# Sixteen of a layer's 32 modulation products moved from the convolution stage into the state-space chunk loop

## What is computed

```python
mod = (jax.nn.silu(c) @ w['w_ada'] + w['b_ada'])[:, None, :]     # w_ada: 1024 x 6144
sh1, sc1, g1, sh2, sc2, g2 = jnp.split(mod, 6, axis=-1)
h = rmsnorm(x, w['ln_mix']) * (1 + sc1) + sh1
q, k, v, qi, ki, wi, z, xbc, dtr, xpool = _split_cols(h @ w['w_in'], IN_SIZES)
a_out = attend(q, k, v, qi, ki, wi)
s_out, new_ssm, new_conv = ssd_mixer(z, xbc, dtr, ...)           # width-4 convolution, chunked state-space scan
p_out, new_pool = pool_mixer(xpool, ...)
x = x + g1 * (jnp.concatenate([a_out, s_out, p_out], axis=-1) @ w['w_out'])
h2 = rmsnorm(x, w['ln_ffn']) * (1 + sc2) + sh2
x = x + g2 * ((jax.nn.silu(h2 @ w['w_gate']) * (h2 @ w['w_up'])) @ w['w_down'])
```

## Time and profile before

| | us |
|---|---|
| median of 3 runs | 3644.96 (3644.76 to 3650.87) |
| the profiled execution | 3638.68 |
| span of its records | 3636.9 |
| mean granted TensorE clock, share of full speed | 0.922 |

### The profile page before, as it was taken

The page is one execution under the profiler, slowest core; times in us unless marked ns, Lnnn a source line. Parts: engine busy times, 40 slices in busy tenths (PEclk is TensorE's granted clock), DMA queues, the critical chain, the costliest instruction groups (busy, mean ns, idle before and its releaser), DMA issues.

```text
span 3636.9 us, 58311 instructions
## 1 busy us (share of the span) xinstructions
PE 3195.1 (88%) x20553; PEld 2728.6 (75%) x20553; DVE 1590.9 (44%) x3481; ACT 1181.4 (32%) x2077; POOL 258.2 (7%) x319
## 2 busy tenths in 40 slices
PE   3997787788889999999989877877888999999995
PEld 2995533265889999999979744334568999999994
DVE  3425568974342222322353265888634323222223
ACT  3222247764332212112131222686532321211211
POOL 1001032102000000000000102210020000000000
PEclk8998779897989999999989976999979999999997
DMA  5125035303311111111122232440151111111111
GB/s 184 38 43 197 21 106 174 105 2 122 111 35 46 42 51 45 41 48 45 41 49 45 87 142 83 139 157 7 48 169 41 41 44 49 46 42 51 46 41 48
DMA packets 275989, 261.18 MB, mean 72 GB/s; under 512 B 85512, under 2 KB 237566, under 8 KB 274512
## 3 DMA queue, kind: packets, MB, share of 16 engines
q1 hardware_dynamic: 244496, 155.76, 14.3%
q0 software_dynamic: 31312, 103.20, 8.8%
HBM read 249.33 MB, written 9.78 MB: 71 GB/s over the span
## 4 chain that ended last, share of the span: by engine, by line
PE 77%; DVE 8%; issue 6%; ACT 4%; DMA 3%; DVEq 0%; another core or an unknown queue 0%; POOL 0%; ACTq 0%; SPq 0%; POOLq 0%
PE bank L723 55%; PE bank L686 5%; PE bank L760 3%; DMA weights<-in_w_ada 2%; ACT arena L1444 2%; PE bank L1123 2%; PE bank L1097 2%; DVE arena L1938 2%; PE bank L1186 1%; PE bank L971 1%; DMA arena<-in_x_sample 1%; PE bank L1145 1%; PE bank L833 1%; PE bank L1063 1%; PE bank L739 1%
## 5 line engine op out<-in xcount | busy, mean ns | idle before, releaser
L723 PE MATMUL bank<-h_hi,w_hi 128*128 128x352 f32 x2784 | 903.2, 324 | 4.5 <-DVE w_lo L1567 4.5
L723 PE MATMUL bank<-h_lo,w_hi 128*128 128x352 f32 x2784 | 893.1, 321 | 0.0
L723 PE MATMUL bank<-h_hi,w_lo 128*128 128x352 f32 x2784 | 892.3, 321 | 0.0
L723 PEld LDWEIGHTS bank<-h_hi,w_hi 128*128 128x128 f32 x2784 | 522.8, 188 | 6.9 <-issue 5.1
L723 PEld LDWEIGHTS bank<-h_lo,w_hi 128*128 128x128 f32 x2784 | 523.6, 188 | 1.7
L723 PEld LDWEIGHTS bank<-h_hi,w_lo 128*128 128x128 f32 x2784 | 522.4, 188 | 0.0
L1567 DVE TENSOR_TENSOR w_lo<-weights,w_hi 128x1024 fp32r<-128x1024 f32 x188 | 230.2, 1225 | 609.6 <-ACT w_hi L1267 603.7
L723 PE MATMUL bank<-g_hi,w_hi 128*128 128x352 f32 x1392 | 451.1, 324 | 5.5 <-DVE arena L629 5.5
L723 PE MATMUL bank<-g_lo,w_hi 128*128 128x352 f32 x1392 | 448.1, 322 | 0.0
L723 PE MATMUL bank<-g_hi,w_lo 128*128 128x352 f32 x1392 | 447.6, 322 | 0.0
L686 PEld LDWEIGHTS bank<-arena 128*128 128x128 f32 (+4 forms) x1773 | 218.1, 156 | 239.3 <-issue 184.3
(11 more groups left out here) (330 smaller groups left out, 3725.7 us busy)
## 6 DMA issues: line engine op xcount, KB each, us to landing
weights<-in_w_ada SPq DMA_DIRECT2D x64, 512.0 KB, 6.8
weights<-in_w_gate SPq DMA_DIRECT2D x44, 512.0 KB
weights<-in_w_up SPq DMA_DIRECT2D x44, 512.0 KB, 3.8
weights<-in_w_in SPq DMA_DIRECT2D x72, 256.0 KB, 3.5
arena<-in_w_ada SPq DMA_DIRECT2D x32, 512.0 KB
weights<-in_w_down SPq DMA_DIRECT2D x32, 448.0 KB, 3.6
arena<-in_w_ada SPq DMA_DIRECT2D x8, 1024.0 KB, 18.2
weights<-in_w_down SPq DMA_DIRECT2D x16, 512.0 KB, 3.8
```

The costliest lines, as they stand in the source:

```text
L723: mm = pe.matmul(bank[:, 0:TC], wt[:, w], xt[:, x], start=(k + m == 0), stop=(k == n_k - 1 and m == 2))
```

## The change

Stage 4 keeps the first sixteen loads (row 1), and ScalarE copies them out after all four Silus and not between the second and third. The other sixteen (row 2) are multiplied in stage 5, two behind the `outputs` of each of the eight full chunks, the last two of them ahead of the transposes of the final state. They accumulate in a bank of their own, `GB`, which is bank 2; the ring `A` has only banks 0 and 1 in that stage. Row 2 is copied out and turned at the end of stage 5, through another place in SBUF (`O_ADAT2`). TensorE's loop of three turns over pairs of chunks becomes straight code. SyncE's program is the same: it issues a load as soon as the buffer six loads ahead is free. VectorE's and GpSimd's programs stay as they were.

```diff
-        AB_FEW, DB_MORE = psum[0:2], psum[2:6]
+        AB_FEW, DB_MORE, GB = psum[0:2], psum[2:6], psum[2]
-        O_ADAT = R(23, 512)
+        O_ADAT, O_ADAT2 = R(23, 512), R(25, 512)
...
-                for u in range(ADA_EARLY):
-                    if u == 2 * KD:
-                        pe.wait_ge(ada_rows, l * 3 + 2)
-                        modulation_turn(l * 3 + 2)
+                def modulation_part(u, into=YB):
+
                     pe.wait_ge(ada_full[u % 6], l * (16 * ((ADA_EARLY + 5 - u % 6) // 6)) + 16 * (u // 6 + 2))
-                    modulate(O_ADAE[u % 6], u // 2 % KD, u % 2).then_inc(w_empty, 1)
-                modulation_turn(l * 3 + 3)
+                    modulate(O_ADAE[u % 6], u // 2 % KD, u % 2, into).then_inc(w_empty, 1)
+
+                for u in range(2 * KD):
+                    modulation_part(u)
+                modulation_turn(l * 3 + 2)
...
                 Dr.restart()
+                A.use(AB_FEW)
                 decays(0, 0, P, C("upper"), C("ones"))
                 settle(pe)
-                with loop(pe, NB // 2 - 1, counts) as i:
-                    for t in range(2):
-                        decays(i * 2, t + 1, P, C("upper"), C("ones"))
-                        outputs(i * 2, t)
-                decays(0, NB - 1, P, C("upper"), C("ones"))
-                outputs(0, NB - 2)
+                for c in range(NB - 1):
+                    if c % 2 == 0 and c < NB - 2:
+                        Dr.pos = 3
+                    decays(c - c % 2, c % 2 + 1, P, C("upper"), C("ones"))
+                    outputs(c - c % 2, c % 2)
+                    for u in range(2):
+                        modulation_part(2 * KD + 2 * c + u, GB)
...
                 outputs(0, NB - 1)
+                for u in range(2):
+                    modulation_part(4 * KD - 2 + u, GB)
                 Dr.wait_read()
...
-                A.restart()
+                modulation_turn(l * 3 + 3, O_ADAT2)
+                A.use(AB)
                 ended(pe, l, 5)
...
                     act.activation(S(R(R_U + i), TOK), S(R(R_U + i), TOK), ACT.Silu)
-                    if i == 1:
-                        modulation_rows(w_empty, l * ADA_USES + 2 * KD)
-                        modulation_columns(1)
-                modulation_rows(w_empty, l * ADA_USES + 4 * KD)
-                modulation_columns(2)
+                modulation_rows(w_empty, l * ADA_USES + 2 * KD)
+                modulation_columns(1)
...
                 exponentials(0, NB, NS)
-                A.restart()
+                modulation_rows(w_empty, l * ADA_USES + 4 * KD, GB, O_ADAT2)
+                modulation_columns(2)
+                A.use(AB)
                 ended(act, l, 5)
```

More of the change, by code:

```diff
@@ L765, in pair_by_tile, with modulate, modulation_turn @@
                 units.n += 2
-            def modulate(at, k, h):
+            def modulate(at, k, h, into=YB):
                 for j in range(4):
-                    mm = pe.matmul(B(YB, [[1, 256]], 256 * h, 32 * j, 32), S(O_CT + 32 * k, 32), S(at + 256 * j, 256),
+                    mm = pe.matmul(B(into, [[1, 256]], 256 * h, 32 * j, 32), S(O_CT + 32 * k, 32), S(at + 256 * j, 256),
                                    start=(k + h == 0), stop=(k + h == KD), skip_group_check=True)
                 return mm
-            def modulation_turn(rows):
+            def modulation_turn(rows, at=O_ADAT):
                 pe.wait_ge(ada_rows, rows)
@@ L779, in modulation_turn @@
                 for c in range(4):
-                    mm = T(B(bank, [[1, P]], P * c), S(O_ADAT + P * c, P))
+                    mm = T(B(bank, [[1, P]], P * c), S(at + P * c, P))
                 A.close(mm)
@@ L1309, in _, with modulation_rows @@
             act.activation(S(R(1), D, 0, 9), S(R(1), D, 0, 9), ACT.Silu).then_inc(c_silu, 1)
-            def modulation_rows(sem, done):
+            def modulation_rows(sem, done, bank=YB, at=O_ADAT):
                 act.wait_ge(sem, done)
-                act.activation(S(O_ADAT, 512), YB[:, :], ACT.Copy).then_inc(ada_rows, 1)
+                act.activation(S(at, 512), bank[:, :], ACT.Copy).then_inc(ada_rows, 1)
             def modulation_columns(r):
```

## The result

The changed kernel takes 3620.86 us (median of four runs, 3618.26 to 3621.77) where the kernel before takes 3647.05 (3644.76 to 3650.87): ratio 0.9926, 95% interval 0.9911 to 0.9942, 26 us less. The changed kernel's profiled execution has a span of 3619.9 us, only 17.0 less than the 3636.9 of before, so 9 of the 26 us are not in this pair of traces at all. Much of what follows is about them.

The account below looks back on a forecast made before the run. TensorE had 77% of the chain, with `w_ada` loads ending stage 4 and ScalarE's staging awaited in stage 5; 9.7 + 6.5 - 0.7 - 2.0 = 13.5 us less, 3625.2 profiled, 3631.5 timed, range 3621 to 3641.

Parts of the forecast that it names:

- The leg of loads: End of stage 4: `w_ada` loads with modulation end last; moving sixteen leaves VectorE's convolution and pooling as the late leg.
- From the mark to the first `decays`: End of stage 4: 0.2 us from VectorE's mark to the first pooling product, then 6.75 to ScalarE's staging, both layers.
- The loads in stage 5: Stage 5: added parts wait for loads in TensorE's queue, but six buffers cover them; costed at nothing.
- rivals C and D: Stage 5 chunk loop: C, TensorE bounds the chain, 3645 us, chance 0.10; D, its clock falls, 3658, chance 0.04.
- 6.5 less 0.7: Stage 5 chunk intervals: filled gaps raise TensorE's clock, 6.5 us gained, less 0.7 for added parts in slow intervals.
- the changed kernel's should stand likewise: Timed runs: the median stands 6.3 us above the profiled execution, so profiled 3625.2 becomes timed 3631.5.
- the term of stage 4: End of stage 4: pooling products begin right behind VectorE's mark; 3.4 us gained in layer 1, 6.3 in layer 2, together 9.7.
- The term with the wrong sign: End of stage 5: parts 30 and 31 ahead of the state's transposes cost 1.0 us in each layer, 2.0 together.
- The added parts at half clock: Stage 5 gaps: two added parts per chunk cost 0.15 us for each interval still at half clock.
- rival D: Stage 5 chunk loop: added parts push it to half clock, 13 us slower, 3658 us; chance 0.04.

Follow-up runs that it names:

- `e_unroll`: The kernel before with only TensorE's loop over pairs of chunks written out as straight code; no product moved or added; ratio to before 0.9997.
- `e_fill_only`: The kernel before, stage 4 untouched, chunk loop as straight code, two modulation parts with unread results behind each chunk's outputs; ratio to before 0.9962.

## Why the forecast was half of the gain

**What was right.** The leg of loads ended stage 4, and VectorE's took its place. From the mark to the first `decays` I had 6.95 us to the staging and so 7.8 to `decays`, 15.6 for both layers; three traces have 15.8 in the mean. The loads in stage 5 hold nobody up. The gap had room: rivals C and D did not come. The clock rose with the added work and gave 7.0 us in the first pair of traces, 8.2 in the mean of all, where 6.5 less 0.7 was forecast. The straight code gives nothing.

**The step that failed: "the changed kernel's should stand likewise".** The profiled execution of before lay 6.3 us under the median of its timed runs and 6.1 under the fastest of them, and I carried the 6.3 over to the changed kernel as an offset common to both. It isn't common. The changed kernel's profiled execution (3621.77) is the highest of its four timed runs, 0.9 us above their median of 3620.86. The forecast for the profiled execution, 3625.2, was 3.4 us too high; the forecast for the timed runs, 3631.5, was 10.6 too high, and 7.2 of these are this step.

Where the first trace of before saved its time isn't settled. Against the three later traces it has 25.3 us from mark to first `decays` in place of 31.6, 30.9 and 30.6. Its clock over that stretch was 0.80 and 0.61, theirs 0.59 to 0.64, and its pooling products began 5.8 and 6.5 us behind VectorE's mark, theirs 7.7 to 8.8. In the changed kernel they begin 0.2 us behind it in every trace, and the whole stretch takes 7.3 to 8.5 us a layer, so what the loads added, and what they varied by, is gone. By the means of all traces the term of stage 4 is 13.8 us where 9.7 were forecast. The longer stretch of the three later traces would account for some 6 us if the timed runs of before on the slower kind of chip had it as well; no trace from such a chip does (25.3, and 23.4 in `e_unroll`). Nor did a low trace save its time in these stages alone: the one of `e_unroll` has a span 7.9 us under that of the first trace of before, and in stages 4 and 5 it is 2.2 us longer.

**The term with the wrong sign: the end of stage 5.** I added 2.0 us for parts 30 and 31 ahead of the state's transposes. From `L922` to `L686` it is 2.28 us in layer 1 and 3.02 in layer 2, where 1.85 were before; so the parts did cost 0.4 and 1.2, near enough. But the whole end got 2.2 shorter in the mean, and the clock was still up when it began: the eight products of the sample chunk's `decays` took 1.07 and 1.08 us (`L905`), and 1.91 and 1.73 before (`L904`). TensorE's timeline in layer 1, before and after:

```profile
430.40 1.91 PE L904 MATMUL bank<-arena 32*128 32x32 f32 x8
424.10 1.07 PE L905 MATMUL bank<-arena 32*128 32x32 f32 x8
```

I had let the gain of the clock end with the sixth interval. `e_fill_only`, with the added products alone, has the end 4.2 us shorter. In the first pair of traces the end is 0.9 shorter, 2.9 us against the forecast, and by the means of all it is 4.2.

**What is left.** The added parts at half clock are a small cost that the forecast set at 0.15 an interval. The stretch from the first to the third `decays` is 0.2 to 0.3 us longer in five of the six layers traced (12.46 for 12.17 in layer 1) and 1.3 in one; TensorE wasn't the one waited for there, but ScalarE's staging, and its cause isn't found. In layer 2 the 3.02 us from `L922` to `L686` stand between the 2.56 of running on and the 3.16 of waiting for the ends at each change of shape, nearer to the latter; and in the gap shown at 380.19 us the parts begin 1.12 us behind `L922`, where running on would be 0.85 and waiting for its end 1.21. With the rule that changing the tiling mode drains the engine (the Trainium skill, TensorEngine Tiling (Array Packing), Key Properties) the trace rather agrees, but two gaps don't decide it.

Against rival D the prediction said that the clock was 1.00 where TensorE was busiest, 3.71 of 4.40 us. That reading is wrong: the same rows have it busy 6.00 of 6.70 us at 0.66. D didn't come all the same.

The sums: forecast 13.5; this pair of traces 17.1 in the two stages (9.8 less 0.6, 7.0, 0.9); mean of all traces 23.3; timed 26.2. Of the missing 12.7 us, 7.2 are the offset carried over, 2.1 the median of before, which a fourth run raised from 3644.96 to 3647.05, and 3.4 the sum itself, of which the end of stage 5 gives 2.9 and the clock of the six intervals 1.2, less 0.6 for the stretch ahead of them. The 9 us by which the timed runs differ more than the two first traces are placed in no trace from the slower kind of chip.

## What to carry to other kernels

If the profiled execution lies under all timed runs by half of the effect that you forecast, don't carry the difference over to the changed kernel: here it was 6.3 us one way and then 0.9 the other. Take a second trace on the same chip before sizing any term, or widen the range to the side on which the change removes what varies. On an engine whose clock follows its work, products moved into gaps of a chain of short bursts may be worth more there than what they free elsewhere: here extra work alone gave 13.6 us. And when a leg of loads is taken off a stage's end, what it varied by goes too: the pooling products began 5.8 to 8.8 us behind VectorE's mark before, and 0.2 after.

## What the runs showed of the hardware that was not expected

The clock of one and the same chunk loop takes several courses: over six intervals, traces of before have 0.84, 0.74, 0.84, 0.84, 0.80, 0.68, 0.77 and 0.76 as the mean of a layer, and single intervals from 5.96 to 8.68 us. At a clock of 1.00 six intervals took 38.6 to 38.7 us in each of eight loops, whether two or four parts stood in the gap. Chips differ, by 55 us for this kernel, nearly all of it in stages that run beside GpSimd's gathers. The stage after stage 6 took 52.2 us in layer 1 of the first trace of before (VectorE's marks at 498.68 and 550.90 us) and 43.6 in the second, and the stretch between its marks at 726.5 and 939.2 us took 212.7 and 198.1; both layers together make 47 us of the 49 between the two traces. In the first trace of the changed kernel, the stage of transposes in layer 2 took 2.6 us longer than in the six other traces of the two kernels; I don't know why.
